# GpSimd's queue reordered: the sums of the next weight tile ahead of the low part of the tile before

## The chip, the cores and the metric

The kernel runs on one core of a Trainium2 chip. The metric is the device time of one launch in microseconds. A core has a matrix engine (TensorE; PE in the profile, with its weight loads as PEld), VectorE (DVE), ScalarE (ACT), GpSimd (POOL) and a queue of transfers on SyncE (SP). Each engine works through its own queue of instructions in the order in which they are written; semaphores order the engines among each other.

## The reference, cut to what matters

One decoder layer for a prompt of 512 rows and a sample group of 8 x 4 rows, 544 token columns in all. The change touches the two feed-forward blocks, each with 1024 features in, 2 x 2816 hidden and 1024 out:

```python
def swiglu(h, w_io, w_o):
    gate, up = jnp.split(h @ w_io, 2, axis=-1)
    return (jax.nn.silu(gate) * up) @ w_o
...
        x = x + 0.5 * swiglu(rms_norm(x, norm_gain[l, 0]), ffn_in[l, 0], ffn_out[l, 0])
        mix, st = token_mixer(...)
        x = x + mix @ w_out[l]
        x = x + 0.5 * swiglu(rms_norm(x, norm_gain[l, 2]), ffn_in[l, 1], ffn_out[l, 1])
```

All is float32. Every product of matrices is done as three products of shorter numbers: each operand is split in a high part (the value rounded to fp32r) and a low part (the rest), and high x high, high x low and low x high are added up.

## The kernel before

A feed-forward block runs through `STEPS`: three groups of 8, 7 and 7 hidden tiles (128 hidden features each, a step of the first layer), and after each group 8 feature steps of the second layer, which read the group's hidden tiles `HIDH` (high) and `HIDL` (low). There are two blocks, f = 0 ahead of the token mixer and f = 1 behind it.

A hidden tile is computed with seven products in place of eight, by sums and differences of the four quarters of the weights and of the tokens (a scheme of the Strassen kind). For one tile s:

- SyncE brings two weight units of 512 KB (L578) into a ring of four raw slots. A unit may be overwritten when the low parts of its own tile are done.
- GpSimd forms four weight sums, `weight_sums(f, s)`: L732, L735, L738, L740. The second and third read the one before. Each goes into one of seven slots of `WP`, which is free when the product of the tile before that used it is done (`part_free`, a wait on `w_used`).
- ScalarE writes the high part of each of the seven weight parts (`part_hi`, L1437) and VectorE the low part (`part_lo`, L1813), in place of the sum, which is why the first two sums' low parts also wait for the sum behind them.
- TensorE makes seven products of 12 matmuls (L938 to L940). Product 1 of tile s waits until the fifth addition of tile s-1 has read its bank.
- VectorE adds the products up in seven additions (L1937, one operand in PSUM, one in SBUF), and after ScalarE's two silu (L1523, L1527) multiplies gate and up (L1956, L1958, both operands in SBUF) into `HIDF`.
- ScalarE writes the high part `HIDH` of the hidden tile (`hid_hi`, L1507), and GpSimd the low part `HIDL` (`hid_lo`, L745), in place of `HIDF`. Only the feature steps at the group's end read `HIDL`.

VectorE's queue in tile s is: L1813 (first part of tile s+1), three L1937, L1813, two L1937, three L1813, two L1937, L1956, L1958, two L1813. GpSimd's queue is, in every step of the first layer, `weight_sums(f, s)` and then `hid_lo(f, s - 1)`. In block 0 it also issues copies of cache rows from DRAM to DRAM (L758), spread over the steps, each behind a wait on `w_used` for the products of the tile before.

Of the kernel before, what the change touches and what calls it, by code (L numbers as in the profile page):

```python
# [49 lines left out]
def ffn_steps():  # L50

    steps, q, u = [], 0, 0
    for first, n in GROUPS:
        for m in range(n):
            steps.append((True, first, n, m, q, u))
            q, u = q + 7, u + 2
        for oc in range(KD):
            steps.append((False, first, n, oc, q, u))
            q, u = q + 2, u + 1
    return steps, q, u  # L60


STEPS, NQ, NRAW = ffn_steps()
NSTEP = len(STEPS)
# [122 lines left out]
def build(nc, I, O):  # L187
    ctx = ExitStack()
    with ctx:
# [198 lines left out]
        def part_slot(q):  # L388
            return PART_SLOT[q % 7]

        def part_free(engine, f, q):

            if q >= 7:
                engine.wait_ge(w_used, Q_FFN[f] + q - 6)
            elif f == 1:
                engine.wait_ge(w_used, L_OUT + (6, 6, 7, 8, 8, 8, 8)[q])
            elif q >= 2:
                engine.wait_ge(m_done, NCH)

        def raw_landed(engine, f, u):  # L400
            engine.wait_ge(landed[u % 4], 16 * ((U_FFN[f] + u) // 4 + 1))

        def tile_no(f, s):
            return FCH * f + STEPS[s][1] + STEPS[s][3]
# [142 lines left out]
        def _(sp):  # L547
# [17 lines left out]
            def ffn_loads(f):  # L565
                w1 = I["ffn_in"][0, f].rearrange("(k p) n -> p k n", p=P)
                w2 = I["ffn_out"][0, f].rearrange("(k p) n -> p k n", p=P)
                read = [q + (7 if first else 2) for first, _, _, _, q, _ in STEPS for _ in range(2 if first else 1)]
                for in_layer1, first, n, x, q, u0 in STEPS:
                    for u in range(u0, u0 + (2 if in_layer1 else 1)):  # L570
                        if u >= 4:
                            sp.wait_ge(w_lo, Q_FFN[f] + read[u - 4])
                        elif f:
                            sp.wait_ge(w_used, L_OUT + (5, 6, 7, 7)[u])
                            sp.wait_ge(w_lo, L_OUT + 5 + u)
                        if in_layer1:
                            c = (first + x) * P + (u - u0) * FF
                            sp.dma_start(RAWF[:, u % 4, :].rearrange("p (k n) -> p k n", k=KD), w1[:, :, c:c + P])\  # L578
                                .then_inc(landed[u % 4], 16)
                        else:  # L580
                            sp.dma_start(RAWF[:, u % 4, 0:n * P].rearrange("p (k n) -> p k n", k=n),
                                         w2[:, first:first + n, x * P:(x + 1) * P]).then_inc(landed[u % 4], 16)
# [30 lines left out]
            def states():  # L613
                def flat(name):
                    return O[name].rearrange("a b t x h d -> (a b) t (x h d)")

                u_p, u_s = O["pool_p"][0, 0], O["pool_s"][0]
                yield O["cmp_s"].rearrange("a b t x h d -> (a b t) (x h d)"), PROJ[0:NS, 4, C_CMP:C_CMP + 256]
                yield u_p, PROJ[P - 15:P, 3, C_U:C_U + 256]
                yield u_s[:, 11:15, :], PROJ[0:NS, 4, C_U:C_U + 256]  # L620
                for name, c in (("slc", C_SLCK), ("win", C_WINK)):
                    yield flat(name + "_p")[0].rearrange("(t p) c -> p t c", p=P), PROJ[:, 0:4, c:c + 256]
                yield O["slc_s"].rearrange("a b t x h d -> (a b t) (x h d)"), PROJ[0:NS, 4, C_SLCK:C_SLCK + 256]
                yield flat("win_s")[:, 508:512, :], PROJ[0:NS, 4, C_WINK:C_WINK + 256]
                for g, (w, _) in enumerate(WDIL):
                    n = min(w, TP) // P
                    for x, c in enumerate((C_KB + g * P, C_VB + g * P)):
                        yield (flat(f"dil{g}_p")[0].rearrange("(t p) c -> p t c", p=P)[:, :, x * P:(x + 1) * P],
                               PROJ[:, 4 - n:4, c:c + P])
                        yield flat(f"dil{g}_s")[:, w - TS:w, x * P:(x + 1) * P], PROJ[0:NS, 4, c:c + P]  # L630
# [67 lines left out]
        def _(pool):  # L698
# [24 lines left out]
            def weight_sums(f, s):  # L723

                _, _, _, _, q, u = STEPS[s]
                done = 4 * tile_no(f, s)
                raw_landed(pool, f, u)
                raw_landed(pool, f, u + 1)
                a11, a12, a21, a22 = (RAWF[:, (u + n // 2) % 4, n % 2 * 512:(n % 2 + 1) * 512] for n in range(4))
                s1, s2, s4, s3 = (WPF[:, part_slot(q + j), 1, :] for j in (1, 2, 3, 4))  # L730
                part_free(pool, f, q + 1)
                nc.gpsimd.tensor_tensor(s1, a21, a22, ALU.add).then_inc(ff["weight_sums"], 1)  # L732
                part_free(pool, f, q + 2)
                pool.wait_ge(ff["weight_sums"], done + 1)
                nc.gpsimd.tensor_tensor(s2, s1, a11, ALU.subtract).then_inc(ff["weight_sums"], 1)  # L735
                part_free(pool, f, q + 3)
                pool.wait_ge(ff["weight_sums"], done + 2)
                nc.gpsimd.tensor_tensor(s4, a12, s2, ALU.subtract).then_inc(ff["weight_sums"], 1)  # L738
                part_free(pool, f, q + 4)
                nc.gpsimd.tensor_tensor(s3, a11, a21, ALU.subtract).then_inc(ff["weight_sums"], 1)  # L740

            def hid_lo(f, s):
                m = STEPS[s][3]
                pool.wait_ge(ff["hid_hi"], tile_no(f, s) + 1)
                nc.gpsimd.tensor_tensor(HIDL[:, m, :], HIDF[:, m, :], HIDH[:, m, :].bitcast(F32), ALU.subtract)                    .then_inc(ff["hid_lo"], 1)  # L745


            ends = [q + (7 if first else 6) for first, _, _, _, q, _ in STEPS]
            spread = lambda before: 14 + (ends[-1] + 30 - 14) * before // copied
            sent = 0  # L750
            for s, (in_layer1, _, _, x, q, _) in enumerate(STEPS):
                if in_layer1:
                    weight_sums(0, s)
                if s and STEPS[s - 1][0]:
                    hid_lo(0, s - 1)
                while (in_layer1 or x < 4) and sent < N_COPIES and spread(pieces[sent][2]) < q + 7:
                    pool.wait_ge(w_used, max(q, 1))
                    pool.dma_start(pieces[sent][0], pieces[sent][1]).then_inc(cpy, 16)  # L758
                    sent += 1
# [36 lines left out]
            def load_slc(b):  # L796

                for t in range(TS):
                    for h in range(2):
                        u = t * KVT + h * 1024  # L800
                        row = b * 8 + h * TS + t
                        pool.indirect_dma_start(KV[b % 2][0:SEL7, u:u + 1024], None, slc_rows,
                                                bass.IndirectOffsetOnAxis(ap=IXS[:, row:row + 1], axis=0))\
                            .then_inc(ld_kv[b % 2][t], 16)
# [16 lines left out]
            for b in range(2, NB):  # L821
                pool.wait_ge(sa["pva"], b - 1)
                load_slc(b)
            for s in range(NSTEP):
                if STEPS[s][0]:
                    weight_sums(1, s)
                if s and STEPS[s - 1][0]:
                    hid_lo(1, s - 1)


        @block.tensor
# [1587 lines left out]
```

## Time and profile before

| what | us |
|---|---|
| median of three runs | 1715.51 (1714.55 to 1717.97) |
| the profiled execution's own time | 1714.78 |
| its span | 1712.4 |
| TensorE busy in the span | 1550.3 (91%) |
| VectorE busy | 1122.6 (66%) |
| ScalarE busy | 755.3 (44%) |
| GpSimd busy | 446.9 (26%) |

The busy share of TensorE is an average, and its matmuls are pipelined (their recorded durations overlap), so it hides short waits; these are read from the starts of its matmuls. The two feed-forward blocks lie at about 300 to 710 us and 1299 to 1702 us of the span. In them the chain of work that ended last often leaves TensorE and runs over GpSimd and VectorE.

### The profile page before, as it was taken

The numbers are of one execution on the slowest core, as the hardware profiler recorded it, in microseconds if no ns is written. First come the engines' busy times: TensorE is split into PE (matmuls) and PEld (weight loads), VectorE is DVE, ScalarE is ACT, GpSimd is POOL, SyncE is SP. The second block draws the span as 40 slices with busy tenths as digits, with TensorE's granted clock in tenths as the row PEclk, the third lists the DMA queues.
The fourth block names the chain that finished last, engine by engine and source line by source line (L and its number), as shares of the span: only waits on it lengthen the run. The fifth ranks groups of instructions, "written<-read, shape, count | busy, mean of one in ns | idle before, by whom it ended". The sixth has DMA issues, their size and how long they took to land.

```text
span 1712.4 us, 28054 instructions
## 1 busy us (share of the span) xinstructions
PE 1550.3 (91%) x10819; PEld 1424.4 (83%) x10819; DVE 1122.6 (66%) x2115; ACT 755.3 (44%) x1508; POOL 446.9 (26%) x375
## 2 busy tenths in 40 slices
PE   4999997898998998999987998999795989989998
PEld 3778886788998998999976776777695989989988
DVE  4777788986587488625547995222359883783872
ACT  4556665443254344323344554455414442442441
POOL 0000000362253263000143002333002641641640
PEclk9999999899999999999977999999996999999999
DMA  8324230155336345233224005889130332332231
GB/s 308 117 113 182 99 141 8 50 197 160 111 125 221 111 146 162 76 125 105 86 94 127 1 1 141 251 256 259 45 99 25 99 111 63 99 101 82 78 111 53
DMA packets 184055, 202.89 MB, mean 118 GB/s; under 512 B 10150, under 2 KB 167565, under 8 KB 181325
## 3 DMA queue, kind: packets, MB, share of 16 engines
q1 hardware_dynamic: 167893, 111.67, 21.2%
q0 software_dynamic: 11680, 89.10, 15.5%
q8 instruction: 87, 1.43, 0.3%
q10 hardware_dynamic: 4352, 0.34, 0.2%
q14 instruction: 43, 0.35, 0.1%
HBM read 195.86 MB, written 31.40 MB: 133 GB/s over the span
## 4 chain that ended last, share of the span: by engine, by line
PE 59%; DVE 13%; POOL 12%; issue 9%; ACT 4%; DMA 2%; SPq 1%; POOLq 0%; DVEq 0%; ACTq 0%; PEldq 0%
PE PS L938 10%; PE PS L940 10%; PE PS L939 10%; PE PS L892 3%; PE PS L894 3%; PE PS L893 3%; PE PS L876 3%; POOL WR L738 3%; DVE WP L1813 3%; POOL WR L732 2%; POOL HIDL L745 2%; POOL WR L735 2%; PE PS L1293 2%; POOL WR L740 2%; PE PS L1221 1%
## 5 line engine op out<-in xcount | busy, mean ns | idle before, releaser
L1813 DVE TENSOR_TENSOR WP<-WR,WP 128x512 fp32r<-128x512 f32 (+1 forms) x404 | 351.3, 896 | 141.5 <-POOL WR L735 64.7
L938 PE MATMUL PS<-TH,WP 128*128 128x272 f32 x1232 | 364.7, 296 | 53.0 <-DVE TL L1900 30.6
L1437 ACT ACTIVATE WP<-WR 128x512 fp32r<-128x512 f32 (+1 forms) x404 | 243.1, 617 | 381.8 <-PE PS L940 133.8
L940 PE MATMUL PS<-TH,WP 128*128 128x272 f32 x1232 | 359.8, 292 | 0.0
L939 PE MATMUL PS<-TL,WP 128*128 128x272 f32 x1232 | 359.1, 291 | 0.0
L938 PEld LDWEIGHTS PS<-TH,WP 128*128 128x128 f32 x1232 | 235.6, 191 | 65.6 <-issue 39.1
L940 PEld LDWEIGHTS PS<-TH,WP 128*128 128x128 f32 x1232 | 236.0, 192 | 0.0
L939 PEld LDWEIGHTS PS<-TL,WP 128*128 128x128 f32 x1232 | 236.0, 192 | 0.0
L938 PE MATMUL PS<-HIDH,WP 128*128 128x272 f32 x704 | 204.3, 290 | 17.5 <-POOL HIDL L745 13.8
L1820 DVE TENSOR_TENSOR PT<-PS,PT 64x512 fp32r<-64x512 f32 x256 | 176.4, 689 | 66.3 <-ACT PT L1444 63.3
L940 PE MATMUL PS<-HIDH,WP 128*128 128x272 f32 x704 | 204.1, 290 | 0.0
L939 PE MATMUL PS<-HIDL,WP 128*128 128x272 f32 x704 | 203.4, 289 | 0.0
L1444 ACT ACTIVATE PT<-PS 64x512 fp32r<-64x512 f32 x256 | 151.8, 593 | 103.1 <-PE PS L876 101.5
L938 PEld LDWEIGHTS PS<-HIDH,WP 128*128 128x128 f32 x704 | 133.2, 189 | 19.8 <-issue 19.8
L732 POOL TENSOR_TENSOR WR<-WR 128x512 f32<-128x512 f32 x44 | 68.5, 1556 | 280.8 <-PE PS L940 157.0
L939 PEld LDWEIGHTS PS<-HIDL,WP 128*128 128x128 f32 x704 | 133.3, 189 | 0.0
L940 PEld LDWEIGHTS PS<-HIDH,WP 128*128 128x128 f32 x704 | 133.1, 189 | 0.0
L745 POOL TENSOR_TENSOR HIDL<-BIG,HIDH 128x544 fp32r<-128x544 f32 x44 | 71.7, 1630 | 215.1 <-ACT HIDH L1507 215.1
L1937 DVE TENSOR_TENSOR BIG<-BIG,PS 128x272 f32<-128x272 f32 x264 | 110.1, 430 | 12.4 <-PE PS L940 9.7
L892 PE MATMUL PS<-PT,CW1H 128*128 128x512 f32 x256 | 114.4, 447 | 2.6 <-DVE PT L1820 2.6
L893 PE MATMUL PS<-PT,CW1H 128*128 128x512 f32 x256 | 101.4, 396 | 0.0
L894 PE MATMUL PS<-PT,CW1L 128*128 128x512 f32 x256 | 101.4, 396 | 0.0
(388 smaller groups left out, 2925.6 us busy)
## 6 DMA issues: line engine op xcount, KB each, us to landing
WR<-in_ffn_in SPq DMA_DIRECT2D x88, 512.0 KB, 4.1
out_dil_s<-in_cache_dil_kv POOLq DMA_DIRECT2D x8, 2044.0 KB, 10.1
WR<-in_ffn_out SPq DMA_DIRECT2D x32, 448.0 KB, 4.2
WR<-in_w_in SPq DMA_DIRECT2D x14, 648.0 KB, 4.9
WR<-in_ffn_out SPq DMA_DIRECT2D x16, 512.0 KB, 4.5
BIG<-in_cache_dil_kv SPq DMA_DIRECT2D x8, 512.0 KB
WR<-in_w_out SPq DMA_DIRECT2D x8, 512.0 KB, 4.3
out_dil_s<-in_cache_dil_kv POOLq DMA_DIRECT2D x8, 508.0 KB, 5.8
```

Source lines behind the costliest of these rows:

```text
L745: nc.gpsimd.tensor_tensor(HIDL[:, m, :], HIDF[:, m, :], HIDH[:, m, :].bitcast(F32), ALU.subtract) .then_inc(ff["hid_lo"], 1)
L892: pe.matmul(out, hi, pt[:, 0, j, :, c:c + 256], start=(q == 0 and x == 0), stop=False)
L893: pe.matmul(out, hi, pt[:, 1, j, :, c:c + 256], start=False, stop=False)
L894: mm = pe.matmul(out, lo, pt[:, 0, j, :, c:c + 256], start=False, stop=(q == 3 and x == 3))
L938: pe.matmul(out, a[0], b[0], start=first, stop=False)
L939: pe.matmul(out, a[0], b[1], start=False, stop=False)
L940: return pe.matmul(out, a[1], b[0], start=False, stop=last)
L1437: act.activation(WP[:, sl, 0, 0:src.shape[-1]], src, ACT.Copy).then_inc(w_hi, 1)
L1444: last = act.activation(PTX[X % 4][p * HD:(p + 1) * HD, 0, :, h, 0:256], PS[h * HD:(h + 1) * HD, 2 * (X % 2) + p, :].rearrange("p (j n) -> ...
L1813: V.tensor_tensor(WP[:, sl, 1, 0:w], src, WP[:, sl, 0, 0:w].bitcast(F32), ALU.subtract).then_inc(w_lo, 1)
L1820: last = V.tensor_tensor(pt[:, 1], src, pt[:, 0].bitcast(F32), ALU.subtract)
L1937: V.tensor_tensor(out, a, PS[:, bank, 0:HALF], ALU.add).then_inc(ff["partial"], 1)
```

## The change

GpSimd's queue alone is written in another order; no instruction is added or removed, and the queues of the four other engines hold the same instructions in the same order as before. In a group, the sums of tile s+1 now stand ahead of the low part of hidden tile s-1. At a group's end the low part of the last tile stands ahead of the first sums of what follows, as it did, and the first sums of a group are written one step earlier, in the last feature step.

```diff
+            def ahead(f, s):
+
+
+                tile_behind = s and STEPS[s - 1][0]
+                if tile_behind and not STEPS[s][0]:
+                    hid_lo(f, s - 1)
+                if s + 1 < NSTEP and STEPS[s + 1][0]:
+                    weight_sums(f, s + 1)
+                if tile_behind and STEPS[s][0]:
+                    hid_lo(f, s - 1)
+
...
+            weight_sums(0, 0)
             for s, (in_layer1, _, _, x, q, _) in enumerate(STEPS):
-                if in_layer1:
-                    weight_sums(0, s)
-                if s and STEPS[s - 1][0]:
-                    hid_lo(0, s - 1)
+                ahead(0, s)
                 while (in_layer1 or x < 4) and sent < N_COPIES and spread(pieces[sent][2]) < q + 7:
...
+            weight_sums(1, 0)
             for s in range(NSTEP):
-                if STEPS[s][0]:
-                    weight_sums(1, s)
-                if s and STEPS[s - 1][0]:
-                    hid_lo(1, s - 1)
+                ahead(1, s)
```

The first place is inside the first group of block 0, on GpSimd. Before: the sums of tile 2 (L732 to L740), the low part of tile 1 (L745), a copy, the sums of tile 3, the low part of tile 2.

```order
L732 TENSOR_TENSOR WR<-WR 128x512
L735 TENSOR_TENSOR WR<-WR 128x512
L738 TENSOR_TENSOR WR<-WR 128x512
L740 TENSOR_TENSOR WR<-WR 128x512
L745 TENSOR_TENSOR HIDL<-BIG,HIDH 128x544
L758 DMA out_dil_s<-in_cache_dil_kv 32x16352
L732 TENSOR_TENSOR WR<-WR 128x512
L735 TENSOR_TENSOR WR<-WR 128x512
L738 TENSOR_TENSOR WR<-WR 128x512
L740 TENSOR_TENSOR WR<-WR 128x512
L745 TENSOR_TENSOR HIDL<-BIG,HIDH 128x544
```

The same stretch of the changed kernel: the sums of tile 2, the low part of tile 0, the sums of tile 3, the low part of tile 1, the copy.

```order
L732 TENSOR_TENSOR WR<-WR 128x512
L735 TENSOR_TENSOR WR<-WR 128x512
L738 TENSOR_TENSOR WR<-WR 128x512
L740 TENSOR_TENSOR WR<-WR 128x512
L745 TENSOR_TENSOR HIDL<-BIG,HIDH 128x544
L732 TENSOR_TENSOR WR<-WR 128x512
L735 TENSOR_TENSOR WR<-WR 128x512
L738 TENSOR_TENSOR WR<-WR 128x512
L740 TENSOR_TENSOR WR<-WR 128x512
L745 TENSOR_TENSOR HIDL<-BIG,HIDH 128x544
L767 DMA out_dil_s<-in_cache_dil_kv 32x16352
```

Between the sums of two tiles there stands one L745 as before, but that of a tile further back, and the copy has moved behind the sums of tile 3.

The second place is the end of the same group and the start of the next, on GpSimd. Before: the low part of the group's last tile, a copy, the sums of the next group's tile 0, those of its tile 1, the low part of its tile 0.

```order
L745 TENSOR_TENSOR HIDL<-BIG,HIDH 128x544
L758 DMA out_dil_s<-in_cache_dil_kv 32x16352
L732 TENSOR_TENSOR WR<-WR 128x512
L735 TENSOR_TENSOR WR<-WR 128x512
L738 TENSOR_TENSOR WR<-WR 128x512
L740 TENSOR_TENSOR WR<-WR 128x512
L732 TENSOR_TENSOR WR<-WR 128x512
L735 TENSOR_TENSOR WR<-WR 128x512
L738 TENSOR_TENSOR WR<-WR 128x512
L740 TENSOR_TENSOR WR<-WR 128x512
L745 TENSOR_TENSOR HIDL<-BIG,HIDH 128x544
```

The changed kernel there: the same start, and the sums of tile 2 behind those of tile 1.

```order
L745 TENSOR_TENSOR HIDL<-BIG,HIDH 128x544
L767 DMA out_dil_s<-in_cache_dil_kv 32x16352
L732 TENSOR_TENSOR WR<-WR 128x512
L735 TENSOR_TENSOR WR<-WR 128x512
L738 TENSOR_TENSOR WR<-WR 128x512
L740 TENSOR_TENSOR WR<-WR 128x512
L732 TENSOR_TENSOR WR<-WR 128x512
L735 TENSOR_TENSOR WR<-WR 128x512
L738 TENSOR_TENSOR WR<-WR 128x512
L740 TENSOR_TENSOR WR<-WR 128x512
L732 TENSOR_TENSOR WR<-WR 128x512
L735 TENSOR_TENSOR WR<-WR 128x512
```

The low part that the features wait for (the first row) keeps its place; the queue behind it differs first at the third set of sums.

## Rows read from the trace of the kernel before

**Rows 1.** Page, part 4: the chain that ended last, shares of the span by engine.

```profile
PE 59%; DVE 13%; POOL 12%; issue 9%; ACT 4%; DMA 2%; SPq 1%; POOLq 0%; DVEq 0%; ACTq 0%; PEldq 0%
```

**Rows 2.** Stretches: us, busy PE, PEld, DVE, ACT, POOL, clock, DMA share, GB/s.

```profile
461.89:540.11 78.22, 75.36 (x590) 74.15 (x588) 64.40 (x104) 39.36 (x74) 45.74 (x33) 1.00 0.43 142
...
483.05:493.62 10.57, 10.57 (x86) 10.57 (x85) 8.94 (x16) 5.06 (x10) 6.12 (x5) 1.00 0.54 183
...
515.99:528.16 12.17, 11.06 (x86) 10.65 (x85) 10.09 (x16) 5.79 (x11) 7.72 (x6) 1.00 0.73 262
```

**Rows 3.** TensorE's timeline where it restarts in a late tile.

```profile
518.34 0.39 PE L938 MATMUL PS<-TH,WP 128*128 128x272 f32 x1 [0.67 <-DVE CKT L1937]
```

**Rows 4.** The chain that ended last, through one tile: start, us, what.

```profile
499.80 1.64 POOL HIDL L745
...
506.46 2.97 DVE WP L1813 x3
...
511.11 0.67 ACT HIDH L1507
...
511.84 0.24 POOL HIDL L745
```

**Rows 5.** GpSimd's wait for the high part, in 461.9 to 710 us: us, times, longest.

```profile
POOL HIDL L745 <- ACT HIDH L1507: 64.3, 14, 7.4
```

**Rows 6.** VectorE's timeline: start, us, what, count [idle before, releaser].

```profile
474.35 0.44 DVE L1958 TENSOR_TENSOR BIG<-GB,BIG 128x272 f32<-128x272 f32 x1
...
510.64 0.43 DVE L1958 TENSOR_TENSOR BIG<-GB,BIG 128x272 f32<-128x272 f32 x1
...
512.32 1.73 DVE L1813 TENSOR_TENSOR WP<-WR,WP 128x512 fp32r<-128x512 f32 x1
513.97 1.37 DVE L1937 TENSOR_TENSOR BIG<-BIG,PS 128x272 f32<-128x272 f32 x3
516.78 0.69 DVE L1813 TENSOR_TENSOR WP<-WR,WP 128x512 fp32r<-128x512 f32 x1 [1.44 <-POOL WR L735]
...
517.85 0.44 DVE L1937 TENSOR_TENSOR CKT<-BIG,PS 128x272 f32<-128x272 f32 x1
518.63 2.97 DVE L1813 TENSOR_TENSOR WP<-WR,WP 128x512 fp32r<-128x512 f32 x3 [0.34 <-POOL WR L738]
...
522.45 0.44 DVE L1956 TENSOR_TENSOR BIG<-GB,CKT 128x272 f32<-128x272 f32 x1
522.80 0.43 DVE L1958 TENSOR_TENSOR BIG<-GB,BIG 128x272 f32<-128x272 f32 x1
...
534.86 0.43 DVE L1958 TENSOR_TENSOR BIG<-GB,BIG 128x272 f32<-128x272 f32 x1
```

**Rows 7.** GpSimd's timeline in the same tile.

```profile
516.89 1.71 POOL L738 TENSOR_TENSOR WR<-WR 128x512 f32<-128x512 f32 x1
518.56 1.29 POOL L740 TENSOR_TENSOR WR<-WR 128x512 f32<-128x512 f32 x1
```

**Rows 8.** GpSimd's timeline in a group's first tile, which TensorE starts at 461.89.

```profile
465.26 1.30 POOL L732 TENSOR_TENSOR WR<-WR 128x512 f32<-128x512 f32 x1 [7.85 <-PE PS L940]
466.70 1.30 POOL L735 TENSOR_TENSOR WR<-WR 128x512 f32<-128x512 f32 x1
468.19 1.30 POOL L738 TENSOR_TENSOR WR<-WR 128x512 f32<-128x512 f32 x1 [0.20 <-PE PS L940]
```

**Rows 9.** VectorE and GpSimd side by side at the start of block 1.

```profile
1315.09 2.37 DVE L1900 TENSOR_TENSOR TL<-BIG,TH 128x1088 fp32r<-128x1088 f32 x1
1317.38 1.77 DVE L1813 TENSOR_TENSOR WP<-WR,WP 128x512 fp32r<-128x512 f32 x1
...
1316.54 2.06 POOL L740 TENSOR_TENSOR WR<-WR 128x512 f32<-128x512 f32 x1 [0.23 <-PE PS L940]
```

**Rows 10.** All instructions of L745: ns min/median/max.

```profile
L745 POOL TENSOR_TENSOR HIDL<-BIG,HIDH x44: 1328/1651/1667, 329.0 to 1660.9; 128x544 fp32r<-128x544 f32 x44
```

**Rows 11.** Weight loads of the first layer, issue to landing.

```profile
DMA to landing us min/median/max: 3.5/4.1/10.7
```

## The prediction

> **What bounds the kernel now.** I read the chain of work first: it is TensorE for 59% of the span, VectorE for 13%, GpSimd for 12% [rows 1]. So in stretches TensorE isn't what the end waits for, and the next view is the busy time by stretch. A tile that nothing hinders takes 10.57 us, its 84 matmuls at 0.126 us; a late one takes 12.17 us with the same matmuls; seven tiles of a group take 78.22 us where 74.0 would do (7 x 10.57). The granted clock is 1.00, the 2.4 GHz level, in all of them, so the loss is waiting [rows 2]. TensorE's own timeline names it: product 1 waits for VectorE's fifth addition of the tile before [rows 3]. VectorE's L1958, one in each tile, comes every 12.1 us (474.35 to 534.86 in five steps) while TensorE is still running at 10.57 [rows 6]. VectorE's side sets the pace, and TensorE is held once it has used up its lead.
>
> Why 12.1? The chain through one tile closes on itself: from one L745 (499.80) to the next (511.84) is 12.04 us, over the sums, three L1813, the rest of the tile, L1507 [rows 4]. L745 stands in GpSimd's queue ahead of the next sums and waits for the tile's high part, up to 7.4 us [rows 5]; the sums come late, and VectorE idles for them 1.44 and 0.34 us in a tile [rows 6]. This ring is what the change cuts: L745 of a tile further back never has to wait, and the sums start when TensorE frees their slots.
>
> **What lies under the ring.** VectorE's tile from 510.64 to 522.80 is 12.16 us [rows 6]. I take out the two idles with the 0.08 us by which its instructions otherwise overlap (1.94), 0.10 by which 512.32 comes later than 510.64 + 0.36 + 0.61 + 0.61 (it waited for ScalarE's part), and two L1813 that took over 1 us more than their 0.69: 512.32 at 1.73 (1.04 more), and three at 2.97 where 0.69 + 2 x 0.61 would do (1.06 more; 0.61 is 0.69 less the overlap) [rows 6]. That leaves 8.0 us of VectorE's own work, under TensorE's 10.57. Left alone it would keep up.
>
> But the two long L1813 are no accident. The first runs beside L745, the second beside L740 (518.56, ended 519.85): it ends at about 520.4, 0.55 us after GpSimd is done [rows 6, 7]. In turn L738, started 0.11 us after an L1813 of 0.69, took 1.71 us in place of 1.30 [rows 6 to 8]. Three in a row show strict turns: L1900 ends at 1317.46, the waiting L740 1.14 us later at 1318.60, the waiting L1813 0.55 us later at 1319.15 [rows 9]. So an L1813 and a GpSimd sum exclude each other; whichever waits is served next, and behind the other's end a sum needs 1.14 us, an L1813 0.55, an L745 about 1.21 (its 1.33 alone less the start) [rows 10]. The additions with an operand in PSUM (L1937) keep their pace beside GpSimd: three take 1.37 at 513.97, while L732 runs [rows 6].
>
> The Trainium skill, "SBUF — State Buffer", section "Who interferes with whom", says the same of a VectorE instruction with two SBUF inputs, and adds that the order of issue decides who blocks. By that rule L1956 and L1958 would be blocked too, and the close race below would go to GpSimd; it would give the time that I forecast. These rows show no L1956 or L1958 beside GpSimd.
>
> **The changed tile, step by step.** t = 0 is the end of the fifth addition (517.85 + 0.44 = 518.29), 0.05 us before product 1 starts (518.34) [rows 3, 6]. That product's result releases the sums: in a group's first tile product 1 starts at 463.40 (461.89 + 1.51) and L732 at 465.26, 1.86 later; with 0.1 for a restarting TensorE, L732 is at 2.01. The others follow 1.44, 2.93 and, one more product on, 4.42 us behind it [rows 8]: at 3.45, 4.94, 6.43. VectorE runs three L1813 and two additions, and L1956 is due at 2.68 (518.63 to 522.45, less the 1.06 waited and the overlap of 0.08) [rows 6].
>
> - L1956 meets L732 (to 3.30) and ends at 3.60: 0.49 us lost, if it excludes GpSimd as L1813 does; its body behind a turn is 0.30 (0.44 less the 0.14 by which 0.69 exceeds 0.55).
> - L1958 starts at 3.52, behind L735's 3.45, waits to 4.75 and ends at 5.05: 1.09 lost.
> - The next L1813 starts at 4.97, L738 at 4.94. Nearly even. If GpSimd is first, L1813 ends at 6.24 + 0.55 = 6.79: 1.13 lost.
> - The next L1813 ends at 8.48 behind L740 (7.93): 1.09 lost. The third, the first of the coming tile, ends at 10.24 behind L745 (8.48 + 1.21 = 9.69): 1.16 lost.
> - Three additions start at 10.16 and take 1.37, an L1813 starts 0.08 before their end, and from its start to the end of the two additions behind it are 1.51 (516.78 to 518.29) [rows 6]: 12.96.
>
> So five waits for GpSimd, 4.96 us, on 8.0 give 12.96 us: slower than the ring's 12.07. If VectorE wins the even race, the same steps end at 11.75. TensorE is held in both.
>
> Which? Starts 0.11 us ahead won for VectorE, 0.07 behind (518.56 and 518.63) lost [rows 6, 7]. The race is at 0.03 behind, nearer to the lost one, and I take it for GpSimd. The 1.09 at L1958, 0.07 behind, rests on the measured side.
>
> **The sum.** A group's length follows VectorE's tiles. Between L1958's there are 7, 6 and 6 steps; the last has no sums beside it and stays. That leaves 32 steps in both blocks. Six of them, the last but one of each group, lose the waits at L1956 and L1958, since there are no sums left: 12.96 - 1.58 = 11.38, -0.69 each, -4.1. Four, the first of the later groups, find VectorE close to its work and stay. The other 22 cost +0.89 each: +19.6. While VectorE falls back in each group there is one tile in which the sums meet the three L1813 as well, for one more turn of 1.05: +6 at most; I take 5. Together about +20.5. The waits at a group's end, for the last L745, stay behind the same chain: 0.
>
> The copies in block 0 are issued up to a tile's length later. The weight loads get less room: a raw slot frees at t = 8.48, the load is needed at 12.96 + 2.01, 6.5 us later, against 4.1 in the median and 10.7 at worst [rows 11]. Where a copy collides, up to 4 us each; 0 taken, since VectorE's lateness gives the loads room too.
>
> Against the profiled execution (1714.78, with a span of 1712.4) this is 1735.3; the median of the runs is 0.7 higher. Forecast: **1735.5**.
>
> **Rivals.**
>
> - *VectorE wins the race.* Steps of 11.75: 22 x -0.32 = -7.0, six last-but-one at 10.17: -11.4, the falling back now 2.2 above the old step: +13 at most. Between -18 and -5; I take -6, with the falling back in full: 1709. It decides from 0.03 us between two starts, which is what speaks for it. 0.27.
> - *The race falls now this, now that way*, or VectorE doesn't settle in one pattern: half of +20 and -6, +7: 1722, with bounds from 1712 to 1730. 0.13.
> - *L1956 and L1958 don't exclude GpSimd.* Then 1.58 of waits go, less one new meeting: about 11.3 a step, -0.8 x 26 and the end steps: -18, 1697. Against it: they have two SBUF operands like L1813. 0.05.
> - *The change does nothing*: the ring isn't cut, as the sums wait for TensorE or loads in its place. The queue order says that L745 can't wait; the sums' release at 2.01 is 5.3 us ahead of the 7.3 at which the ring lets them come (511.84 + 12.07 + 1.64, less 518.29) [rows 4, 6]. 0.02.
> - *Loads become the bound* in block 0 on top of the forecast: +4 for each of up to four copies: to 1750. 0.05.
>
> **How the numbers follow.** Forecast 0.48, others as above. 2 in 10 left out below and above gives 1706 to 1741; the likeliest case alone is 1729 to 1740 (without the turn of falling back +15, with all of it and a late load +24). Within 0.2% (3.4 us, what a measurement of this kernel can tell from none) ends a part of the second case and of the mixed one: 0.02 + 0.05 + 0.03 = 0.10. Faster: 0.22 + 0.05 + 0.01 = 0.28. Slower: 0.62.
>
> **What would show it.** VectorE's tile, L1958 to L1958, at about 12.9 us inside a group (11.7 for the first rival, 11.3 for the third); its waits for GpSimd's L735 gone; L1958 at about 1.5 us in place of 0.43; three of a tile's seven L1813 at about 1.8; GpSimd's wait for ScalarE's high part gone but at the group's ends; TensorE's waits inside tiles up from 1.5 to over 2 us. Wrong if L1956 and L1958 stay at 0.44, or if L1813 right behind L1958 takes 0.68.

## The result, and the profile after

The changed kernel takes 1736.15 us (median of four runs, 1732.81 to 1742.79), the kernel before 1715.31 beside it (1714.55 to 1717.97): a ratio of 1.0124, with a 95% interval from 1.0092 to 1.0155. The change costs 20.8 us. The profiled execution took 1736.16 us, with a span of 1733.8 for 1712.4.

In the changed kernel's line numbers, L1813 is now L1820, L1937 is L1944, L1956 and L1958 are L1963 and L1965, L1507 is L1514, and TensorE's L938 to L940 are L945 to L947; L732 to L745 keep theirs.

Where the loss lies is read first, by stretches. From TensorE's first product of a block to its last feature matmul, the kernel before (us, then busy time of PE, PEld, DVE, ACT, POOL, the granted clock, DMA share and GB/s):

```profile
299.80:710.09 410.29, 379.45 (x2906) 372.70 (x2907) 309.38 (x483) 168.92 (x312) 163.87 (x124) 0.98 0.43 137
1298.69:1701.24 402.55, 379.08 (x2904) 371.59 (x2904) 280.61 (x435) 159.61 (x294) 160.05 (x106) 0.98 0.28 82
```

And the changed kernel:

```profile
300.38:722.02 421.64, 385.10 (x2906) 374.74 (x2907) 344.71 (x483) 164.79 (x312) 162.29 (x124) 0.97 0.42 133
1308.83:1722.62 413.79, 384.06 (x2904) 372.50 (x2904) 317.45 (x435) 155.47 (x294) 154.71 (x106) 0.98 0.27 80
```

Each block is 11.3 us longer. The granted clock is 0.98 in both blocks before, 0.97 and 0.98 after; it is 1.00 in the late tile below, so the loss inside the tiles is waiting, and the lower share in block 0 belongs to the end of one group, shown with the copies further down. The column that moved is VectorE's: 72 us more busy time in the two blocks for the same 918 instructions. GpSimd's is 317.0 us for 323.9, so it has none more. In these views a wait for the other engine's turn is recorded as the duration of the instruction that waits, not as idle time.

The chain that ended last has moved accordingly, from GpSimd and issue to VectorE and TensorE [rows 1]:

```profile
PE 66%; DVE 22%; issue 4%; ACT 3%; DMA 2%; POOL 2%; SPq 1%; POOLq 0%; DVEq 0%; ACTq 0%; PEldq 0%
```

A late tile by windows, against 12.17 us for a late one before [rows 2]; TensorE's work in it is the same 84 matmuls:

```profile
507.75:520.70 12.95, 11.48 (x84) 10.74 (x84) 12.70 (x17) 5.45 (x12) 7.63 (x6) 1.00 0.31 93
```

VectorE is busy for 12.70 of 12.95 us. Its timeline through that tile (start, us, what) answers to [rows 6]:

```profile
507.31 0.44 DVE L1944 TENSOR_TENSOR CKT<-BIG,PS 128x272 f32<-128x272 f32 x1
507.66 1.89 DVE L1820 TENSOR_TENSOR WP<-WR,WP 128x512 fp32r<-128x512 f32 x3
509.47 0.78 DVE L1944 TENSOR_TENSOR BIG<-BIG,PS 128x272 f32<-128x272 f32 x2
510.39 0.94 DVE L1963 TENSOR_TENSOR BIG<-GB,CKT 128x272 f32<-128x272 f32 x1 [0.15 <-ACT GB L1534]
511.26 1.53 DVE L1965 TENSOR_TENSOR BIG<-GB,BIG 128x272 f32<-128x272 f32 x1
512.71 5.27 DVE L1820 TENSOR_TENSOR WP<-WR,WP 128x512 fp32r<-128x512 f32 x3
517.90 1.37 DVE L1944 TENSOR_TENSOR BIG<-BIG,PS 128x272 f32<-128x272 f32 x3
519.19 0.68 DVE L1820 TENSOR_TENSOR WP<-WR,WP 128x512 fp32r<-128x512 f32 x1
519.79 0.43 DVE L1944 TENSOR_TENSOR BIG<-BIG,PS 128x272 f32<-128x272 f32 x1
520.26 0.44 DVE L1944 TENSOR_TENSOR CKT<-BIG,PS 128x272 f32<-128x272 f32 x1
```

GpSimd's timeline beside it, which answers to [rows 7]:

```profile
509.74 1.30 POOL L732 TENSOR_TENSOR WR<-WR 128x512 f32<-128x512 f32 x1 [5.25 <-PE PS L947]
511.18 1.31 POOL L735 TENSOR_TENSOR WR<-WR 128x512 f32<-128x512 f32 x1
512.68 1.30 POOL L738 TENSOR_TENSOR WR<-WR 128x512 f32<-128x512 f32 x1 [0.18 <-PE PS L947]
514.17 1.50 POOL L740 TENSOR_TENSOR WR<-WR 128x512 f32<-128x512 f32 x1 [0.20 <-PE PS L947]
515.63 1.80 POOL L745 TENSOR_TENSOR HIDL<-BIG,HIDH 128x544 fp32r<-128x544 f32 x1
```

The two views have to be laid over each other. VectorE's idle waits for a sum are gone, but L1963, L1965 and the three L1820 at 512.71 now each end just behind an instruction of GpSimd: 0.94 in place of 0.44, 1.53 in place of 0.43, and 5.27 for three that need 1.89 by themselves (507.66). GpSimd's L738 starts 0.04 us ahead of the L1820 (512.676 and 512.713 in the records' own digits) and takes its bare 1.30: it has the turn. The first ring is cut, as the wait of GpSimd for the high part shows; in 461.2 to 722 us there are four left, at group ends, for 14 before [rows 5]:

```profile
POOL HIDL L745 <- ACT HIDH L1514: 34.4, 4, 12.8
```

### The profile page after: what moved, and what is told of

Same layout as the page of the kernel before. It is cut to its first block, busy times and chain, and to the rows that moved or that the text cites. A ratio compares the mean times of both kernels' runs of the same rounds, so it can differ in the third digit from the quotient of the medians.

```text
span 1733.8 us, 28054 instructions
## 1 busy us (share of the span) xinstructions
PE 1558.2 (90%) x10819; PEld 1425.8 (82%) x10819; DVE 1195.4 (69%) x2115; ACT 747.2 (43%) x1508; POOL 440.0 (25%) x375
## 4 chain that ended last, share of the span: by engine, by line
PE 66%; DVE 22%; issue 4%; ACT 3%; DMA 2%; POOL 2%; SPq 1%; POOLq 0%; DVEq 0%; ACTq 0%; PEldq 0%
PE PS L945 13%; PE PS L947 12%; PE PS L946 12%; DVE WP L1820 9%; PE PS L899 3%; PE PS L901 3%; PE PS L900 3%; PE PS L883 3%; DVE BIG L1944 2%; PE PS L1300 2%; PE PS L1253 1%; PE PS L1228 1%; PE PS L1276 1%; DVE TL L1907 1%; DMA WR<-in_ffn_out 1%
## 5 line engine op out<-in xcount | busy, mean ns | idle before, releaser
L1820 DVE TENSOR_TENSOR WP<-WR,WP 128x512 fp32r<-128x512 f32 (+1 forms) x404 | 389.8, 997 | 89.4 <-ACT WP L1444 59.9
L945 PE MATMUL PS<-TH,WP 128*128 128x272 f32 x1232 | 368.8, 299 | 66.3 <-DVE TL L1907 30.0
L947 PE MATMUL PS<-TH,WP 128*128 128x272 f32 x1232 | 359.6, 292 | 0.0
L1444 ACT ACTIVATE WP<-WR 128x512 fp32r<-128x512 f32 (+1 forms) x404 | 234.5, 612 | 239.2 <-PE PS L947 135.0
L945 PEld LDWEIGHTS PS<-TH,WP 128*128 128x128 f32 x1232 | 235.7, 191 | 87.7 <-issue 46.1
L947 PEld LDWEIGHTS PS<-TH,WP 128*128 128x128 f32 x1232 | 236.0, 192 | 0.0
L945 PE MATMUL PS<-HIDH,WP 128*128 128x272 f32 x704 | 204.3, 290 | 15.9 <-POOL HIDL L745 15.9
L947 PE MATMUL PS<-HIDH,WP 128*128 128x272 f32 x704 | 204.6, 291 | 0.0
L732 POOL TENSOR_TENSOR WR<-WR 128x512 f32<-128x512 f32 x44 | 59.5, 1352 | 432.7 <-PE PS L947 308.8
L945 PEld LDWEIGHTS PS<-HIDH,WP 128*128 128x128 f32 x704 | 133.5, 190 | 17.1 <-issue 17.0
L947 PEld LDWEIGHTS PS<-HIDH,WP 128*128 128x128 f32 x704 | 133.5, 190 | 0.0
L1944 DVE TENSOR_TENSOR BIG<-BIG,PS 128x272 f32<-128x272 f32 x264 | 110.1, 430 | 15.0 <-PE PS L947 12.3
L745 POOL TENSOR_TENSOR HIDL<-BIG,HIDH 128x544 fp32r<-128x544 f32 x44 | 74.8, 1699 | 93.3 <-ACT HIDH L1514 93.3
```

Source lines behind the costliest of these rows:

```text
L945: pe.matmul(out, a[0], b[0], start=first, stop=False)
L947: return pe.matmul(out, a[1], b[0], start=False, stop=last)
L1444: act.activation(WP[:, sl, 0, 0:src.shape[-1]], src, ACT.Copy).then_inc(w_hi, 1)
L1820: V.tensor_tensor(WP[:, sl, 1, 0:w], src, WP[:, sl, 0, 0:w].bitcast(F32), ALU.subtract).then_inc(w_lo, 1)
L1944: V.tensor_tensor(out, a, PS[:, bank, 0:HALF], ALU.add).then_inc(ff["partial"], 1)
```

## The experiments

Times are medians with the lowest and highest run; the kernel before ran beside each set, at 1714.97 us (20 runs, 1708.42 to 1721.49) for the first four, 1714.40 (14 runs, 1709.90 to 1726.65) for the next four and 1715.62 (24 runs, 1707.69 to 1724.09) for the last four. The ratios are the record's and need not be the quotients of these medians. A tile is the step from one end of L1965 to the next; each kernel was profiled once, and tiles and stops are those of that execution.

The theory is the prediction's: GpSimd's instructions and those of VectorE with two operands in SBUF exclude each other in turns, and the early sums meet five of VectorE's.

### Block 1 alone

```diff
             def ahead(f, s):
+                if f == 0:
+                    if STEPS[s][0] and s:
+                        weight_sums(f, s)
+                    if s and STEPS[s - 1][0]:
+                        hid_lo(f, s - 1)
+                    return
```

> Block 0 has the old order, block 1 the new one; block 1 has no copies. The theory (GpSimd and VectorE shut each other out, five waits in each tile): VectorE's tile is 12.06 us in block 0 and 12.94 in block 1, and block 1 alone gives its share of the loss, +11 us: about 1726.5. The rival (the loss comes from the copies and loads, which block 0 alone has together): no change, 1715 to 1717.

Measured: 1723.93 us (1722.72 to 1734.30, 7 runs), 1.0065 of the kernel before (1.0039 to 1.0091). The two blocks in its profiled execution:

```profile
299.33:708.38 409.05, 380.88 (x2906) 374.14 (x2907) 309.69 (x483) 168.84 (x312) 164.42 (x124) 0.97 0.43 138
1297.53:1711.18 413.65, 382.00 (x2904) 370.48 (x2904) 318.75 (x435) 155.54 (x294) 155.28 (x106) 0.99 0.27 80
```

Block 0 is as before, and block 1, which has no copies, takes 413.65 us, 11.1 more than the 402.55 of before. Its tiles are at 12.95. The median is 2.6 us under the forecast and far from the rival's: the copies aren't needed for the loss.

### The third sum held back until VectorE is through

```diff
                 pool.wait_ge(ff["weight_sums"], done + 2)
+                if s >= 2 and STEPS[s - 1][0] and STEPS[s - 2][0]:
+                    pool.wait_ge(bank_free[f], s + 1)
                 nc.gpsimd.tensor_tensor(s4, a12, s2, ALU.subtract)
```

> The new order, and inside a group the third sum (L738) also waits for the gate's last product (L1965) of the hidden tile two before, so that VectorE's L1820 behind it starts first. The theory: the even race is turned, VectorE's tile falls from 12.94 to 11.7 us and the last but one from 11.35 to 10.15; about 1709, below both kernels, with bounds of 1704 and 1716 from how a group's second tile falls back. The rival (VectorE is late for another reason than the turns, such as TensorE's release of the sums): the third sum only comes 0.1 us later, and the time stays at 1736 or rises.

Measured: 1709.76 us (1701.35 to 1713.25, 12 runs), 0.9960 of the kernel before (0.9942 to 0.9978). The tiles are 11.77 us and the last but one 10.17, as forecast; the second of each later group still takes 13.5 to 14.0. One wait more on GpSimd takes 26 us off the changed kernel: GpSimd started too early, not too late.

### The products of gate and up without a second operand in SBUF

```diff
-                        V.tensor_tensor(HIDF[:, x, HALF:T], GB[:, s % 2, 1, :], SUM4, ALU.mult)
+                        V.tensor_tensor(HIDF[:, x, HALF:T], GB[:, s % 2, 1, :], PS[:, 7, 0:HALF], ALU.mult)
...
-                        V.tensor_tensor(HIDF[:, x, 0:HALF], GB[:, s % 2, 0, :], SUM2, ALU.mult)
+                        V.tensor_tensor(HIDF[:, x, 0:HALF], GB[:, s % 2, 0, :], PS[:, 7, 0:HALF], ALU.mult)
```

> The new order; the two products of gate and up read a fixed bank of PSUM in place of up's sum, so the multiplication by up is left out of the result. The theory (two operands in SBUF are what shuts GpSimd out): L1963 and L1965 take 0.44 us each beside a sum, their waits of 0.49 and 1.09 us go, and VectorE's tile is about 11.3 us; 26 tiles at -1.6 us and the rest of each group give 1693 to 1700. The rival (only L1820, with its output written over its own operand, excludes GpSimd, and the two products are slow for another reason): both stay at 0.95 and 1.53 us, and the time at 1736.

Measured: 1700.86 us (1688.09 to 1702.26, 4 runs), 0.9888 (0.9849 to 0.9926), with tiles of 11.28. VectorE's timeline in one of them:

```profile
510.06 0.44 DVE L1963 TENSOR_TENSOR BIG<-GB,PS 128x272 f32<-128x272 f32 x1 [0.15 <-ACT GB L1534]
510.41 0.43 DVE L1965 TENSOR_TENSOR BIG<-GB,PS 128x272 f32<-128x272 f32 x1
510.76 2.38 DVE L1820 TENSOR_TENSOR WP<-WR,WP 128x512 fp32r<-128x512 f32 x2
```

And GpSimd's:

```profile
509.43 1.29 POOL L732 TENSOR_TENSOR WR<-WR 128x512 f32<-128x512 f32 x1 [2.93 <-PE PS L947]
510.85 1.74 POOL L735 TENSOR_TENSOR WR<-WR 128x512 f32<-128x512 f32 x1
```

L1963 runs from 510.06 to 510.50 wholly inside L732 and both keep their bare durations. The same instruction with its second operand in SBUF took 0.94 there. The L1820 behind, started 0.09 ahead of L735, keeps its turn, and L735 takes 1.74. So it is the second operand in SBUF that excludes, and GpSimd pays when it is the one behind. The Trainium skill, "SBUF — State Buffer", section "Who interferes with whom", says so of both kinds: with at most one SBUF input, and outside its modes that use two ports, a VectorE instruction doesn't contend with GpSimd; with two it does, if GpSimd reads SBUF. The measurements agree, 0.44 and 0.94 us.

### The copies ahead of the sums

The issue of a copy moves from behind `ahead(0, s)` into it, ahead of `weight_sums(0, s + 1)`:

```diff
                 if tile_behind and not STEPS[s][0]:
                     hid_lo(f, s - 1)
+                in_layer1, _, _, x, q, _ = STEPS[s]
+                while f == 0 and (in_layer1 or x < 4) and sent[0] < N_COPIES and spread(pieces[sent[0]][2]) < q + 7:
+                    pool.wait_ge(w_used, max(q, 1))
+                    pool.dma_start(pieces[sent[0]][0], pieces[sent[0]][1]).then_inc(cpy, 16)
+                    sent[0] += 1
                 if s + 1 < NSTEP and STEPS[s + 1][0]:
                     weight_sums(f, s + 1)
```

> The new order, with each copy of block 0 issued ahead of the sums of the next tile, which is when the old order issued it. The theory: the copies have no part in the 12.94 us of a tile; the stop at the group's end that lies in the second group of block 0 (7.6 us) goes back to the first (5.4 us), and the time is 1732 to 1736. The rival (later copies are the cost): at least 8 us come back, 1728 or less.

Measured: 1730.27 us (1728.91 to 1731.20, 4 runs), 1.0085 (1.0058 to 1.0112), 2 us below the band expected and 2 above the rival's. The tiles stay at 12.94 to 12.97. The stop at a group's end (the longest gap between two of TensorE's matmuls there) is 1.7 to 1.8 us in all six groups, where the changed kernel had 7.6 in one: so 6 us came back, and none of it in the tiles.

### All sums held back

The same wait as in the second experiment, ahead of the first sum (L732) in place of the third.

> The new order, and inside a group all four sums of a tile wait for the gate's last product (L1965) of the hidden tile two before. The theory: L1963 and L1965 meet no sum, VectorE's tile is 11.5 us in place of 12.94, also the one in which VectorE falls back (14.0), about 14 us under the old kernel: 1701, with bounds of 1697 and 1706. The rival (a sum that starts later than TensorE allows must make TensorE wait, since the new order's own gain is that it starts early): at least as slow as the new order, 1736 or more.

Measured: 1703.77 us (1696.16 to 1711.59, 7 runs), 0.9915 (0.9885 to 0.9945). The tiles are 11.53 to 11.58, none falls back, and L1963 and L1965 are at 0.44 in all 44. The first sum starts 3.95 us behind the fifth addition in place of 2.00. Sums that start 1.95 us later make the kernel 32 us faster.

### The third sum beside the additions

```diff
                 pool.wait_ge(ff["weight_sums"], done + 2)
+                if s >= 2 and STEPS[s - 1][0] and STEPS[s - 2][0]:
+                    pool.wait_ge(w_lo, Q_FFN[f] + q + 1)
                 nc.gpsimd.tensor_tensor(s4, a12, s2, ALU.subtract)
```

> The new order, and inside a group the third sum waits until VectorE has done the first low part (L1820) of its own tile, behind which stand the three additions with an operand in PSUM, 1.37 us. The theory: L1965's wait stays, but the third sum lies beside the additions, and three of VectorE's five waits are left or shortened: a tile of about 10.8 us, 1690, with bounds of 1685 and 1700. The rival (the additions are slowed by a sum beside them, or the fourth sum comes too late for TensorE): tiles of 11.5 us or more, 1705 and above.

Measured: 1686.62 us (1681.64 to 1697.48, 6 runs), 0.9844 (0.9807 to 0.9881). The tiles are 10.92 to 10.96 us in block 1, apart from the second of each later group, which still takes 13.2 to 13.5, and from 10.2 to 11.9 in the first group of block 0. GpSimd's and VectorE's timelines around the third sum, which this kernel has at L740, with L1946 for the additions:

```profile
1348.60 1.29 POOL L740 TENSOR_TENSOR WR<-WR 128x512 f32<-128x512 f32 x1 [2.76 <-DVE WP L1822]
```

```profile
1348.35 1.38 DVE L1946 TENSOR_TENSOR BIG<-BIG,PS 128x272 f32<-128x272 f32 x3
1349.64 0.80 DVE L1822 TENSOR_TENSOR WP<-WR,WP 128x512 fp32r<-128x512 f32 x1
```

The sum takes 1.29 and the three additions 1.38 side by side, as each does alone; only the low part behind them waits, 0.12 us. The rival's two conditions don't occur.

### The low part of the hidden tile beside additions too

```diff
                 if tile_behind and STEPS[s][0]:
+                    if s + 1 < NSTEP and STEPS[s + 1][0]:
+                        pool.wait_ge(w_lo, Q_FFN[f] + STEPS[s + 1][4] + 5)
                     hid_lo(f, s - 1)
```

> As the run before, and the low part of the hidden tile (L745) in GpSimd's queue also waits until VectorE has done the three low parts in a row, so that it lies beside the sixth and seventh addition. The theory: VectorE's tile of 10.9 us, the group's second tile no longer 14.0 but about 11.2, and TensorE's lost time in the tiles of both blocks about 10 to 15 us: 1682, with bounds of 1677 and 1692. The rival (the second hold only moves a turn elsewhere): no faster than the run before.

Measured: 1686.62 us (1679.33 to 1693.00, 6 runs), 0.9841 (0.9813 to 0.9869): the same median as without it, so on the time the rival holds. Both groups of 7 in block 1 now lose nothing in TensorE's tiles, but they had lost only 0.4 us with the run before. Counted from the first to the last matmul start of each group's tiles, against 10.575 us a tile, TensorE loses 32 us in both runs, where 10 to 15 were expected here: 15 us of it in each block's first group. So the gain expected over the run before wasn't there: in the groups of 7 TensorE's own 10.57 us set the pace already, and the loss in the first groups stayed. The group's second tile did fall, to 11.0 us, but the third rose to 12.2 in block 1. The turns weren't all gone either. The first of gate's and up's products takes 0.90 us in most tiles, and the second 1.5 us and more in over a dozen, which is a move of the turn as the rival has it.

### The sums cut short

```diff
-                nc.gpsimd.tensor_tensor(s1, a21, a22, ALU.add).then_inc(ff["weight_sums"], 1)
+                nc.gpsimd.tensor_tensor(s1[:, 0:8], a21[:, 0:8], a22[:, 0:8], ALU.add).then_inc(ff["weight_sums"], 1)
...
-                    src = WPF[:, sl, 1, :]
+                    src = RAWF[:, (u + (j - 1) // 2) % 4, (j - 1) % 2 * 512:((j - 1) % 2 + 1) * 512]
```

The other three sums are cut alike, and the source is changed for ScalarE's high and VectorE's low part.

> The new order with GpSimd's sums cut to 8 of 512 columns; the weight parts 2 to 5 are taken from the raw weights in place of the sums, so the sums are left out of the result. Every semaphore and every other instruction is as in the new order. The theory: without the four long sums VectorE has only L745 to meet and keeps up with TensorE at 10.57 us a tile, so nearly all of the 84 us that TensorE loses in the tiles come back: 1645 to 1660. The rival (part of the loss is TensorE's own, in restarts and in the order of its products, or ScalarE's): tiles stay above 11.3 us, 1690 or more.

Measured: 1654.66 us (1651.33 to 1656.76, 4 runs), 0.9650 (0.9619 to 0.9681). A tile inside a group by windows:

```profile
474.70:485.20 10.50, 10.50 (x86) 10.50 (x85) 8.55 (x17) 5.83 (x12) 2.13 (x5) 1.00 0.35 102
```

VectorE has the same 17 instructions as in the window at 507.75 and is busy 8.55 us, not 12.70; TensorE never waits in it. VectorE and ScalarE keep up by themselves. Counted as above, TensorE loses 18 us in the tiles of this kernel, 9 in the first group of each block and none in the others, where the changed kernel loses 84: those 18 us aren't the long sums' doing. The run doesn't tell exclusion from a GpSimd that is simply slow; that is what the runs before it told.

### Both holds, with the copies ahead

The edits of the fourth, sixth and seventh experiment together.

> The two holds on GpSimd (third sum behind the first low part, L745 behind the three low parts in a row), and the copies ahead of the sums of the next tile. The theory: the copies' place costs nothing in the tiles, and the stops at the group ends of block 0 (1 to 7 us in the runs so far) are smaller when the copies start earlier: 1680 to 1686. The rival (those stops are a matter of chance, whatever the place): 1686 as without it.

Measured: 1691.64 us (1686.45 to 1693.89, 6 runs), 0.9851 (0.9821 to 0.9881). No better than without the copies moved: 5 us above it by the medians, the ratios (0.9851 and 0.9841) within each other's interval. In the profiled execution block 0's group ends stop 4.9, 5.9 and 1.9 us, so the even 1.7 of the fourth experiment wasn't a property of the copies' place.

### Both orders without the copies of block 0

```diff
                     pool.wait_ge(w_used, max(q, 1))
-                    pool.dma_start(pieces[sent][0], pieces[sent][1]).then_inc(cpy, 16)
                     sent += 1
```

> The new order with the 18 copies of block 0 left out (their rows of the cache outputs are not written); their waits on TensorE stay. The theory: block 0 becomes like block 1, with 42.7 us lost in the tiles and 5.3 us in the features, 8 us less than with copies: 1728. The rival (the copies and loads are part of the 12.94 us of a tile): tiles of 12 us in block 0, 1720 or less.

> The old order with the same 18 copies left out. The theory: block 0 becomes like block 1, 28.9 us lost in the tiles and 7.8 us in the features: 1707, so that old and new order stand 22 us apart without copies, as 20.8 us with them. The rival (the copies carry the difference of the orders): 12 us apart or less.

Measured: 1730.04 us (1726.90 to 1731.36, 5 runs) for the new order, 1709.74 (1707.24 to 1713.89, 10 runs) for the old. They stand 20.3 us apart, as 20.8 with copies. The new order's group ends stop 1.65 to 1.75 us each, in all six. The copies cost either order some 6 us, and no part of the difference between them that these runs can tell.

### Three waits that hold nothing back

```diff
                 pool.wait_ge(ff["weight_sums"], done + 2)
+                for _ in range(3):
+                    pool.wait_ge(ff["weight_sums"], done + 2)
                 nc.gpsimd.tensor_tensor(s4, a12, s2, ALU.subtract)
```

> The new order with three more waits ahead of the third sum (L738), on a semaphore that is already at its value: they hold nothing back and only take GpSimd's sequencer some time. The theory (whoever of L1820 and L738 starts first has its turn first, and 0.04 us decide): if the waits delay L738 by 0.05 us or more, VectorE's L1820 wins in most tiles, the tiles fall from 12.94 to about 11.8 us, and the time to 1710 to 1715. The rival (GpSimd has the right of way in a near tie, or the turn is decided by the order of the queues): tiles stay at 12.94 or rise by the delay, 1736 to 1740.

Measured: 1710.18 us (1702.24 to 1716.67, 10 runs), 0.9971 of the kernel before (0.9946 to 0.9995) and 26 us under the changed kernel, from which it differs by instructions that do nothing. GpSimd's and then VectorE's timeline; the third sum is at L740 here, the low part at L1822:

```profile
510.43 1.31 POOL L735 TENSOR_TENSOR WR<-WR 128x512 f32<-128x512 f32 x1
512.00 1.81 POOL L740 TENSOR_TENSOR WR<-WR 128x512 f32<-128x512 f32 x1 [0.26 <-PE PS L949]
```

```profile
510.51 1.53 DVE L1967 TENSOR_TENSOR BIG<-GB,BIG 128x272 f32<-128x272 f32 x1
511.96 4.09 DVE L1822 TENSOR_TENSOR WP<-WR,WP 128x512 fp32r<-128x512 f32 x3
```

The third sum starts 0.26 us behind the second in place of 0.18, and that is behind VectorE's low part at 511.96. Now the sum takes 1.81 and VectorE's three 4.09 in place of 5.27. The tiles are 11.78.

## Why the prediction was right

Forecast 1735.5, measured 1736.15, by the case given the largest chance, inside its own range, and by its mechanism: five waits of VectorE for GpSimd in a tile. Its sum can be laid beside the measured ends of L1965 and L1958, group by group. The two blocks together are 22.6 us longer, the time between them and ahead of them 1.2 shorter, which makes the 21.4 of the span.

| part | forecast | measured |
|---|---|---|
| 22 steps inside groups | +19.6 | +17.2 |
| the additional turn while VectorE falls back | +5 | +4.1 in 4 steps, +3.2 in the blocks' first tiles |
| 6 steps last but one | -4.1 | -4.8 |
| 4 first steps of later groups | 0 | -0.3 |
| 6 last steps | 0 | -0.6, all of it in one step of block 0 |
| group ends | 0 | 0.0 in block 1, +3.7 in block 0 |

That the total is within 0.7 us is in part luck. The parts are off by -2.4 (steps), +2.3 (falling back and first tiles), -0.7, -0.3, -0.6 and +3.7, and the time outside the blocks, for which nothing was forecast, by -1.2: together +0.8. The forecast itself isn't exactly its sum either: 1735.3 from the profiled execution becomes 1736.0 with the 0.7 us by which the median is higher, and 1735.5 lies between the two.

- **The five waits.** Of the steps inside groups in which nothing falls back, 17 of 18 are 12.87 to 12.96 us long, forecast 12.96. Each instruction stands where the step-by-step working had it: L732 2.00 us behind the fifth addition (forecast 2.01), L1963 ends at 3.59 (3.60), L1965 at 5.04 (5.05), the three L1820 at 6.77, 8.47 and 10.23 (6.79, 8.48, 10.24), counted from 507.75.
- **The 22 steps.** 0.89 each was right for block 1 (0.87 to 0.90). It was less in block 0 for two reasons that the forecast didn't have: two steps of the kernel before were at 12.62 already, and in one tile of the changed kernel (at 367.71 us) L735 came 0.5 us late, behind TensorE, so that L1965 got through ahead of it and the step was 11.86. The same tile is late by the same 0.5 us in the runs of the second experiment and without copies; no run shows why.
- **L1956 and L1958 exclude GpSimd**, which no row of before showed. Taken away, 11.28 us a tile and 1700.86; the rival's number was about 11.3 and 1697.
- **The race.** Forecast 0.03 us behind, measured 0.028 to 0.044 behind in 23 tiles, all lost. Turned in two different ways it gives tiles of 11.77 and 11.78 (rival 11.75) and 1709.76 and 1710.18 (rival 1709). So the rival's 0.27 was well placed: less than 0.05 us lie between the two outcomes. That the working came out on the right side has luck in it: the 2.01 us at which it has L732 contain 0.1 us "for a restarting TensorE" for which it names no row, and that is three times the 0.03 us by which it decides.
- **The falling back** was sized for all groups at once; each later group has one tile of 14.0, and each block's first tile takes 1.6 us more.
- **The copies.** The forecast put 0. The stops at the group ends of block 0 were 5.4, 2.4 and 1.8 us in the execution of before and 1.7, 7.6 and 2.4 in that of after. They aren't tied to the order: block 0 of the first experiment, in the old order, has 1.7, 2.9 and 2.4. Without copies the old order is 5.6 us faster and the new one 6.1, so in the medians the forecast's 0 stands. The prediction allowed up to 4 us where a copy collides, and one such stop cost 8.2 us, as shown below; the two profiled executions differ by 3.7 us in these stops. Whether a stop depends on the execution or on the kernel's timing isn't shown.

How such a stop arises is shown by ScalarE's timeline at the end of the changed kernel's second group, which TensorE's tiles leave at 543.0:

```profile
551.50 0.63 ACT L1444 ACTIVATE WP<-WR 128x512 fp32r<-128x512 f32 x1 [6.37 <-DMA WR<-in_ffn_out]
552.04 0.64 ACT L1514 ACTIVATE HIDH<-BIG 128x544 fp32r<-128x544 f32 x1
```

The high part of the group's last hidden tile (L1514), for which the features wait, stands in ScalarE's queue behind the high part of a weight whose load is late: issued at 538.7, it landed at 551.5, and for 9.4 of these 12.7 us a copy of 2044 KB was under way (539.5 to 548.9). In the fourth experiment that copy was issued earlier and landed at 541.7; the same load, issued at 540.3, landed at 546.0, and the stop was 1.7 us. No run moved L1514 ahead of it.

The stop costs more than its own length, through TensorE's clock. TensorE stood still from 546.5 to 554.2 us; the windows view from 549.3 to 559.5:

```profile
549.30:559.50 10.20, 5.27 (x23) 5.30 (x24) 3.49 (x4) 2.22 (x4) 1.33 (x1) 0.50 0.59 176
```

The granted clock is 0.50, the 1.2 GHz level, in this stretch and 1.00 on both sides of it, so TensorE's first 5.3 us of work after the stop ran at the lower level. From the group's last L1965 to the first one of the next group it is 61.9 us, against 53.7 in the kernel before, whose stop there was 2.4 us, and in the run without copies (1.7): 8.2 us more for 5.8 us more of stop than without copies. That is the 0.97 of block 0.

## What to carry to other kernels

Two engines whose instructions exclude each other in turns have a schedule, not only loads. Starting the one earlier can put its instructions exactly where the other can't give way, and what is then lost stands inside the other's durations, where no view of idle time shows it. Lay the two timelines over each other, mark which instructions exclude each other, and give each long one a place beside the other's PSUM work; one semaphore wait did that here, for 1686.6 us against 1715. Where two starts lie within 0.05 us, any edit in the neighbourhood may decide 26 us, as it did here, so put the order down by a wait rather than leave it to timing.

## What was not expected of the hardware

- Three satisfied waits of GpSimd's queue delayed its next instruction by 0.08 us, and a start only 0.002 us ahead of the sum's was enough for VectorE to have the turn (478.64 us in that run: L1822 0.68, the sum 1.83).
- The change of turn lies between starts 0.002 us ahead and 0.024 behind. In the changed kernel and in the one with three more waits, 55 of the 88 tiles have the two starts within 0.13 us of each other: VectorE's low part 0.12 to 0.002 us ahead of the third sum won each time, and 0.028 to 0.066 us behind it lost each time. The first and the fourth experiment have starts 0.024 us behind, also lost.
- The execution-to-execution scatter of this kernel (1707.7 to 1726.7 us for the one before, over 58 runs) is larger than its first runs showed (1714.55 to 1717.97).
- A stop of 7.6 us at a group's end was followed by 5.3 us of work at the 1.2 GHz level.
